# Turns of the logits tile issued ahead of the copies: other turns stand between the turning of a tile and its router product

## The chip, the cores and the metric

The kernel runs on one core of a Trainium2 chip. Its time is the device time of one execution in microseconds (us). The profile is one execution of the same program with the hardware profiler on. The engines are PE (TensorE, matrix products and transposes), DVE (VectorE), ACT (ScalarE), POOL (GpSimd) and SP (SyncE, which here only issues transfers).

## The reference, cut to what matters

The program is one encoder layer on 2048 rows of width 1024, followed by a mixture of experts. The part that the change touches is the *mixing stage*: the outcome of the convolution is normed, the state-space outcome is gated, both are projected and added to the input, and of the new rows the router's logits are computed.

```python
y = layer_norm(y, ln_g, ln_b)                   # convolution branch: norm over 512 channels
y_conv = jax.nn.silu(y)
y = jax.nn.gelu(y).astype(u.dtype)              # state-space branch
y_ssm = y * jax.nn.sigmoid(y @ glu_w + glu_b)
y_cat = jnp.concatenate([rms_norm(y_conv, gb[:CONV_WIDTH]),
                         rms_norm(y_ssm, gb[CONV_WIDTH:])], axis=-1)
x = x + y_cat @ w_out[l]
h = rms_norm(x, g_ffn[l])
g_logits = xf @ w_rg.astype(f32) + b_rg.astype(f32)   # 4 groups; xf is h, flat
e_logits = xf @ w_re.astype(f32) + b_re.astype(f32)   # 32 experts
```

## The kernel before, in words

Three stages come one after the other: projection and tables, convolution with the state-space part, then mixing (`mix`, from L1101), and behind them the experts. The mixing stage works in eight steps n = 0 to 7 of 256 rows each, held as channels by rows, and a ninth turn of the loop, n = 8, that only finishes. Each step ends in two tiles of 128 rows: tile q = 2n is the first and q = 2n + 1 the second one of step n. The loop is shifted: in turn n of the loop the front of step n is computed together with the output of step n - 1, that is, of tiles 2n - 2 and 2n - 1. Every engine runs its own list of instructions, written out by hand in this order, and waits on semaphores by number; no scheduler reorders anything.

What PE does in turn n of the loop (`body`, L1673), in steady state:

- `ln_in(n)` (L1581): 8 turns (transposes of 128x128) of the convolution's outcome `conv_in` into the PSUM banks pa and pb, so that DVE can take mean and variance of each row.
- `sums(n-1)` (L1617): in every second turn the ranks of the chosen experts, then four products with one column each for the branch norms of the step before. They write the bank pd, where the logits also stand, and so wait until DVE has read the last logits (`logit_read`).
- `out_tile` (L1637) of tile 2n - 2: 48 products of 512 columns, the output projection.
- `logit` (L1655) of tile 2n - 3: 8 turns of the normed rows `h` into pc and pa; ACT copies both banks to `hT` in SBUF (L1379, a copy of each bank); then 8 products of 36 columns give the logits in pd.
- `ln_out(n)` (L1591): 8 turns of the rows that ACT normed (`yn`), into pb and pc, from which ACT computes the swish (L1345).
- `glu(n)` (L1601): 48 products of 256 columns for the gate, into pa and pb. They read `yg_hi` (a cast by ACT, L1338) and `yg_lo` (a difference by DVE, L1487).
- `out_tile` of tile 2n - 1, and `logit` of tile 2n - 2.

ACT's list has, around the odd tile: norming (L1333), the two copies of the turned tile, the cast of `yg`, the swish. DVE's list has there: `yg_lo`, four adds of the output tile (L1510, L1513), the norm of tile 2n - 2, the reading of the logits (L1528), in turns 3, 5 and 7 the choice of experts for four tiles (`choose`, L1449), and then the lows of both branches (L1491, L1499), four adds, the reading of the next logits, the norm of the second tile, and at the start of the next turn the statistics with their root (L1463) that ACT's norming waits for.

There are four small banks (pa, pb, pc, pd) and four for the output projection. The waits that guard the banks are `glu_sig` (ACT has read the gate from pa or pb), `yn_done` (ACT has read the turned inputs), `yc_done` (ACT has read the turned normed rows), `h_copied` (ACT has copied a turned half of a tile).

Of the kernel before, what the change touches and what calls it, by code (L numbers as in the profile page):

```python
# [25 lines left out]
T8 = 8  # L26
# [1068 lines left out]
def wait(engine, sem, value):  # L1095

    if not isinstance(value, int) or value > 0:
        engine.wait_ge(sem, value)


def mix(nc, scratch, ident, routing, x, w_out, g_branch, glu_w, columns, g_ffn, w_router, b_router):  # L1101
# [3 lines left out]
    with ExitStack() as ctx:  # L1105
# [42 lines left out]
        pa, pb, pc, pd = ps("pa"), ps("pb"), ps("pc"), ps("pd")  # L1148
# [8 lines left out]
        ln_tr, ln_own, ln_scale, yn_done, ln_back = (sem(n) for n in ("ln_tr", "ln_own", "ln_scale", "yn_done", "ln_back"))  # L1157
# [5 lines left out]
        h_turned, h_copied, logit_done, logit_read = (sem(n) for n in ("h_turned", "h_copied", "logit_done", "logit_read"))  # L1163
# [5 lines left out]
        block = ctx.enter_context(nc.Block())  # L1169
        PARAMS = 3  # L1170

        def over_steps(engine, body):
            for n in range(T8 + 1):
                body(n, n % 2)
# [8 lines left out]
        def first(n):  # L1183
            return isinstance(n, int) and n == 0

        def last_step(n):
            return isinstance(n, int) and n == T8
# [6 lines left out]
        def _(sp):  # L1194
# [40 lines left out]
            def body(n, par):  # L1235
# [5 lines left out]
                if not first(n):  # L1241
                    for t in range(2):
# [4 lines left out]
                        if not last_step(n):  # L1247
                            sp.dma_start(x_sb[:, t], x_rows[n][t]).then_inc(x_ld[t], 16)
            over_steps(sp, body)
            for t in range(2):  # L1250
                sp.wait_ge(x2_st[t], 16 * T8)
# [72 lines left out]
        def _(act):  # L1324
# [48 lines left out]
                nc.scalar.activation(h[:, t], x2[:, t], ACT.Square, accum_out=st[:, 3, 3:4]).then_inc(x2_sq, 1)  # L1373

            def logit(q, t):
                for b, bank in enumerate((pc, pa)):
                    act.wait_ge(h_turned, q * 2 + b + 1)
                    wait(act, logit_done, q)
                    nc.scalar.copy(hT[:, 4 * b:4 * b + 4, :].rearrange("p c k -> p (c k)"), bank[:, :]).then_inc(h_copied, 1)  # L1379
# [9 lines left out]
            def body(n, par):  # L1389
# [8 lines left out]
                if not first(n) and not (isinstance(n, int) and n == 1):  # L1398
                    logit(n * 2 - 3, 1)
# [180 lines left out]
        def _(pe):  # L1580
            def ln_in(n):  # L1581
                pe.wait_ge(conv_ld, 16 * (n + 1))
                wait(pe, glu_sig, n * 2)
                if not (isinstance(n, int) and n < 2):
                    pe.wait_ge(h_copied, n * 4 - 6)
                for t, bank in enumerate((pa, pb)):
                    for c in range(CT):
                        last = nc.tensor.transpose(bank[:, c * P:(c + 1) * P], conv_in[:, c, t * P:(t + 1) * P], ident[:, :])
                    last.then_inc(ln_tr, 1)

            def ln_out(n):  # L1591
                pe.wait_ge(yn_done, n + 1)
                wait(pe, yc_done, n * CT)
                for b, bank in enumerate((pb, pc)):
                    for c in (2 * b, 2 * b + 1):
                        for t in range(2):
                            at = (c % 2) * TN + t * P
                            last = nc.tensor.transpose(bank[:, at:at + P], yn[:, t, c * P:(c + 1) * P], ident[:, :])
                    last.then_inc(ln_back, 1)

            def glu(n):  # L1601
                pe.wait_ge(yg_lo_done, n + 1)
                if first(n):
                    pe.wait_ge(w_lo_done, 2)
                for b, bank in enumerate((pa, pb)):
                    if b == 1:
                        pe.wait_ge(yc_done, n * CT + 2)
                    for m in (2 * b, 2 * b + 1):
                        o = bank[:, (m % 2) * TN:(m % 2 + 1) * TN]
                        for c in range(CT):  # L1610
                            ms = slice(m * P, (m + 1) * P)
                            nc.tensor.matmul(o, glu_hi[:, c, ms], yg_hi[:, c], start=c == 0, stop=False)
                            nc.tensor.matmul(o, glu_hi[:, c, ms], yg_lo[:, c], start=False, stop=False)
                            last = nc.tensor.matmul(o, glu_lo[:, c, ms], yg_hi[:, c], start=False, stop=c == CT - 1)
                    last.then_inc(glu_done, 1)

            def sums(n):  # L1617
                if not first(n):
                    pe.wait_ge(logit_read, n * 2 - 1)
                if ranked_in(n + 1):  # L1620
                    rank_of((n - 3) // 2)
                pe.wait_ge(summed, n * 2 + 2)
                for t in range(2):
                    for branch in range(2):
                        last = nc.tensor.matmul(pd[:, 2 * t + branch:2 * t + branch + 1], sq[:, branch, 0, t * P:(t + 1) * P],
                                                ones[:, :], start=True, stop=True)
                last.then_inc(sums_done, 1)
# [24 lines left out]
                            last = nc.tensor.matmul(o[:, :], cat_hi[:, par, k, ts], wo_lo[:, k, sl], start=False, stop=c == CT - 1)  # L1652
                    last.then_inc(out_done, 1)

            def logit(q, t, sums_n):  # L1655
                pe.wait_ge(h_done, q + 1)
                for b, bank in enumerate((pc, pa)):
                    for c in range(4 * b, 4 * b + 4):
                        last = nc.tensor.transpose(bank[:, (c % 4) * P:(c % 4 + 1) * P], h[:, t, c * P:(c + 1) * P], ident[:, :])
                    last.then_inc(h_turned, 1)  # L1660
                if q == 0:
                    pe.wait_ge(params, 16 * PARAMS)
                pe.wait_ge(h_copied, q * 2 + 2)
                pe.wait_ge(sums_read, sums_n)
                wait(pe, rank_read, (sums_n - 2) // 2)
                wait(pe, logit_read, q)
                for c in range(KD):
                    last = nc.tensor.matmul(pd[:, 64:64 + NL], hT[:, c], wr[:, c], start=c == 0, stop=c == KD - 1)
                last.then_inc(logit_done, 1)
# [1 line left out]
            pe.wait_ge(ones_done, 1)  # L1671

            def body(n, par):  # L1673
                if not last_step(n):
                    ln_in(n)
                if not first(n):
                    sums(n - 1)
                    out_tile(n * 2 - 2, n - 1, 0, 1 - par)
                    if not (isinstance(n, int) and n == 1):
                        if not last_step(n):  # L1680
                            pe.wait_ge(yn_done, n + 1)
                        logit(n * 2 - 3, 1, n)
                if not last_step(n):
                    ln_out(n)
                    glu(n)
                if not first(n):
                    out_tile(n * 2 - 1, n - 1, 1, 1 - par)
                    if not last_step(n):
                        pe.wait_ge(yc_done, n * CT + CT)
                        pe.wait_ge(glu_sig, n * 2 + 1)  # L1690
                    logit(n * 2 - 2, 0, n)
            over_steps(pe, body)
            logit(2 * T8 - 1, 1, T8)


G0, U0, G1, U1, D0, D1 = range(6)
# [686 lines left out]
```

## Time and profile before

| | us |
|---|---|
| median of 3 runs | 1797.01 |
| lowest, highest | 1789.78, 1798.05 |
| the profiled execution | 1796.61 |
| its span in the trace | 1795.1 |
| PE busy of the span | 1613.8 (90%) |
| DVE busy | 1131.2 (63%) |
| ACT busy | 824.6 (46%) |
| POOL busy | 632.0 (35%) |

The span is cut into stages by the lines that run: the mixing stage reaches from about 508 us to 873 us, and its steady turns from 583 us on. A row of a timeline gives the start and the length of one group of equal instructions; matmuls are pipelined, and a group's start is when its first one is issued, so that starts are compared with starts. The granted clock (PEclk) is a share of full speed: 1.00 is 2.4 GHz and 0.50 is 1.2 GHz, and a value between is a stretch that had both.

### The profile page before, as it was taken

How to read it: one execution, taken by the hardware profiler on the slowest of the kernel's cores; microseconds unless marked ns; L12 is line 12 of the kernel's file. 1: busy time of each engine (PE TensorE's matmuls, PEld its weight loads, DVE VectorE, ACT ScalarE, POOL GpSimd, SP SyncE). 2: the span in 40 equal slices, each digit the busy share in tenths (PEclk: the TensorE clock that was granted, in tenths of full speed). 3: DMA queues.
4: the chain of work that ended last, by engine and by line, in shares of the span. 5: the costliest groups of instructions: out<-in, count | busy, mean ns of one | idle time of the engine just before them, and what ended most of it. 6: DMA issues, size and time to landing. Idle time of an engine off the chain costs nothing.

```text
span 1795.1 us, 32279 instructions
## 1 busy us (share of the span) xinstructions
PE 1613.8 (90%) x11107; PEld 1484.5 (83%) x11108; DVE 1131.2 (63%) x1689; ACT 824.6 (46%) x1024; POOL 632.0 (35%) x895
## 2 busy tenths in 40 slices
PE   6999999699947999999379999999999999999990
PEld 6989898588946888887269999999999999999990
DVE  6766654365457676665446747654665888655576
ACT  3412221036354333342325646654665877655563
POOL 0777767343334235554342222222222121222210
PEclk9999999889968999998689999999999999999995
DMA  8723342498563234322469878796887999888888
GB/s 278 229 103 126 118 154 72 144 259 269 171 220 118 94 106 131 95 82 94 165 191 335 291 246 286 265 326 193 276 268 270 374 400 389 289 257 288 291 267 342
DMA packets 125955, 398.20 MB, mean 222 GB/s; under 512 B 33470, under 2 KB 60480, under 8 KB 98880
## 3 DMA queue, kind: packets, MB, share of 16 engines
q1 hardware_dynamic: 101712, 329.97, 50.5%
q0 software_dynamic: 20480, 58.84, 13.3%
q10 hardware_dynamic: 3696, 8.50, 1.2%
q8 instruction: 42, 0.69, 0.2%
q14 instruction: 25, 0.20, 0.0%
HBM read 311.27 MB, written 85.99 MB: 221 GB/s over the span
## 4 chain that ended last, share of the span: by engine, by line
PE 41%; DMA 5%; issue 2%; DVE 1%; ACT 1%; DVEq 1%; POOL 0%; SPq 0%; POOLq 0%; ACTq 0%
PE moe_p_y L2285 4%; PE moe_p_y L2288 4%; PE moe_p_y L2286 4%; PE moe_p_g0u L2272 4%; PE moe_p_g0u L2270 4%; PE moe_p_g0u L2271 4%; PE moe_p_x L2262 2%; PE moe_p_u L2272 2%; PE moe_p_g L2272 2%; PE moe_p_u L2270 2%; PE moe_p_g L2270 2%; PE moe_p_g L2271 2%; PE moe_p_u L2271 2%; DMA residual<-moe_y,moe_ids_s 2%; DMA moe_more<-residual 1%
## 5 line engine op out<-in xcount | busy, mean ns | idle before, releaser
L1724 DVE TENSOR_TENSOR expert_lo<-expert_raw,expert_hi 128x2048 fp32r<-128x2048 f32 x192 | 433.1, 2284 | 59.5 <-ACT expert_hi L1720 40.3
L1720 ACT CAST expert_hi<-expert_raw 128x2048 fp32r<-128x2048 f32 x192 | 362.0, 1912 | 16.4 <-DMA expert_raw<-in_experts 8.7
L706 PE MATMUL proj_p_z<-proj_x_hi,proj_w_hi 128*128 128x256 f32 x768 | 224.3, 292 | 13.9 <-DVE proj_x_lo L554 13.9
L707 PE MATMUL proj_p_z<-proj_x_lo,proj_w_hi 128*128 128x256 f32 x768 | 219.9, 286 | 0.0
L708 PE MATMUL proj_p_z<-proj_x_hi,proj_w_lo 128*128 128x256 f32 x768 | 219.7, 286 | 0.0
L2270 PE MATMUL moe_p_g0u<-expert_hi,moe_xh 128*128 128x256 f32 x736 | 211.0, 287 | 1.5 <-DVE moe_xl L2138 1.5
L2271 PE MATMUL moe_p_g0u<-expert_hi,moe_xl 128*128 128x256 f32 x736 | 207.0, 281 | 0.0
L2272 PE MATMUL moe_p_g0u<-expert_lo,moe_xh 128*128 128x256 f32 x736 | 206.9, 281 | 0.0
L706 PEld LDWEIGHTS proj_p_z<-proj_x_hi,proj_w_hi 128*128 128x128 f32 x768 | 150.0, 195 | 20.5 <-issue 19.4
L2028 POOL DMA_INDIRECT residual<-moe_y,moe_ids_s x45 | 74.4, 1654 | 228.5 <-ACT moe_y L2069 228.5
L2285 PE MATMUL moe_p_y<-expert_hi,moe_hh 128*128 128x512 f32 x368 | 153.4, 417 | 0.0
L707 PEld LDWEIGHTS proj_p_z<-proj_x_lo,proj_w_hi 128*128 128x128 f32 x768 | 150.2, 196 | 0.1
L708 PEld LDWEIGHTS proj_p_z<-proj_x_hi,proj_w_lo 128*128 128x128 f32 x768 | 149.9, 195 | 0.0
L2286 PE MATMUL moe_p_y<-expert_lo,moe_hh 128*128 128x512 f32 x368 | 144.8, 393 | 0.0
L2270 PEld LDWEIGHTS moe_p_g0u<-expert_hi,moe_xh 128*128 128x128 f32 x736 | 139.6, 190 | 4.0 <-issue 1.9
L2271 PEld LDWEIGHTS moe_p_g0u<-expert_hi,moe_xl 128*128 128x128 f32 x736 | 141.0, 192 | 2.0
L2272 PEld LDWEIGHTS moe_p_g0u<-expert_lo,moe_xh 128*128 128x128 f32 x736 | 139.5, 190 | 0.0
L2019 POOL DMA_DIRECT2D moe_ids_s<-slot_table x46 | 25.8, 562 | 275.9 <-DMA residual<-moe_y,moe_ids_s 275.5
L2288 PE MATMUL moe_p_y<-expert_hi,moe_hl 128*128 128x512 f32 x368 | 115.8, 395 | 0.0
L1650 PE MATMUL mix_p_out<-mix_wo_hi,mix_cat_hi 128*128 128x512 f32 x256 | 105.6, 412 | 0.0
L2069 ACT ACTIVATE moe_y<-moe_p_y,moe_ids_s 128x512 f32<-128x512 f32 x90 | 60.3, 688 | 97.7 <-PE moe_p_y L2288 55.8
L2144 DVE TENSOR_TENSOR moe_hid<-moe_p_u,moe_sil 128x256 f32<-128x256 f32 x46 | 19.5, 423 | 135.7 <-PE moe_p_u L2272 126.1
(431 smaller groups left out, 4210.0 us busy)
## 6 DMA issues: line engine op xcount, KB each, us to landing
expert_raw<-in_experts SPq DMA_DIRECT2D x192, 1024.0 KB
ffn_input<-mix_h SPq DMA_DIRECT2D x17, 512.0 KB, 3.9
proj_x_sb<-in_x SPq DMA_DIRECT2D x8, 1024.0 KB, 8.7
turns<-proj_turn POOLq DMA_DIRECT2D x16, 512.0 KB, 4.5
cs_tw<-turns SPq DMA_DIRECT2D x16, 512.0 KB, 8.7
mix_x_sb<-in_x SPq DMA_DIRECT2D x16, 512.0 KB, 5.0
residual<-mix_x SPq DMA_DIRECT2D x16, 512.0 KB, 2.7
proj_x_raw<-in_x_turned SPq DMA_DIRECT2D x7, 1024.0 KB, 6.5
```

What stands on the lines that cost most here:

```text
L706: nc.tensor.matmul(o, whi, x_hi[:, half, c], start=start, stop=False)
L707: nc.tensor.matmul(o, whi, x_lo[:, half, c], start=False, stop=False)
L708: return nc.tensor.matmul(o, wlo, x_hi[:, half, c], start=False, stop=stop)
L1650: nc.tensor.matmul(o[:, :], cat_hi[:, par, k, ts], wo_hi[:, k, sl], start=c == 0, stop=False)
L1720: self.nc.scalar.copy(self.hi[:, u], self.raw[:, u]).then_inc(self.hi_done, 1)
L1724: tensor_tensor(self.lo[:, u], self.raw[:, u], self.hi[:, u].bitcast(FP32), ALU.subtract).then_inc(self.lo_done, 1)
L2270: nc.tensor.matmul(out, xh[:, c], w_hi, start=c == 0, stop=False)
L2271: nc.tensor.matmul(out, xl[:, c], w_hi, start=False, stop=False)
L2272: last_mm = nc.tensor.matmul(out, xh[:, c], w_low, start=False, stop=c == KD - 1)
L2285: nc.tensor.matmul(p_y[i][:, :], hh[:, c], w_hi, start=c == 0, stop=False)
L2286: nc.tensor.matmul(p_y[i][:, :], hh[:, c], w_low, start=False, stop=False)
L2288: last_mm = nc.tensor.matmul(p_y[i][:, :], hl[:, c], weights.outer(hi, D0 + i, c), start=False, stop=c == F // P - 1)
```

## The change

`logit` on PE is split into `turn_tile` (the 8 turns) and `logit` (the wait for both copies and the 8 products). Between them now stand other turns: in turns 2 to 7 of the loop, behind the odd tile 2n - 3, those of `ln_out(n)`; behind the even tile 2n - 2, for n = 1 to 6, those of `ln_in(n+1)`, which so far opened the next turn of the loop. For this to be free of conflicts on the banks, the order of the banks changes: an even tile is turned into pa first and then pc, an odd one as before into pc and then pa (`turned_banks`, on PE and for ACT's copies alike); `ln_in` fills pb first and then pa, and waits before pa for the first copy of the tile; `ln_out` fills pb and then pc, and waits before pc for the first copy. The lists of DVE, POOL and SP are unchanged, and of ACT's only the order of the two banks for even tiles. No instruction is added or removed.

```diff
@@ -1169,6 +1169,10 @@
         block = ctx.enter_context(nc.Block())
         PARAMS = 3
 
+        def turned_banks(q):
+
+            return (pc, pa) if q % 2 else (pa, pc)
+
         def over_steps(engine, body):
             for n in range(T8 + 1):
                 body(n, n % 2)
@@ -1373,7 +1377,7 @@
                 nc.scalar.activation(h[:, t], x2[:, t], ACT.Square, accum_out=st[:, 3, 3:4]).then_inc(x2_sq, 1)
 
             def logit(q, t):
-                for b, bank in enumerate((pc, pa)):
+                for b, bank in enumerate(turned_banks(q)):
                     act.wait_ge(h_turned, q * 2 + b + 1)
                     wait(act, logit_done, q)
                     nc.scalar.copy(hT[:, 4 * b:4 * b + 4, :].rearrange("p c k -> p (c k)"), bank[:, :]).then_inc(h_copied, 1)
@@ -1581,9 +1585,9 @@
             def ln_in(n):
                 pe.wait_ge(conv_ld, 16 * (n + 1))
                 wait(pe, glu_sig, n * 2)
-                if not (isinstance(n, int) and n < 2):
-                    pe.wait_ge(h_copied, n * 4 - 6)
-                for t, bank in enumerate((pa, pb)):
+                for t, bank in ((1, pb), (0, pa)):
+                    if t == 0 and n > 1:
+                        pe.wait_ge(h_copied, n * 4 - 7)
                     for c in range(CT):
                         last = nc.tensor.transpose(bank[:, c * P:(c + 1) * P], conv_in[:, c, t * P:(t + 1) * P], ident[:, :])
                     last.then_inc(ln_tr, 1)
@@ -1592,6 +1596,8 @@
                 pe.wait_ge(yn_done, n + 1)
                 wait(pe, yc_done, n * CT)
                 for b, bank in enumerate((pb, pc)):
+                    if b == 1 and n > 1:
+                        pe.wait_ge(h_copied, n * 4 - 5)
                     for c in (2 * b, 2 * b + 1):
                         for t in range(2):
                             at = (c % 2) * TN + t * P
@@ -1652,12 +1658,14 @@
                             last = nc.tensor.matmul(o[:, :], cat_hi[:, par, k, ts], wo_lo[:, k, sl], start=False, stop=c == CT - 1)
                     last.then_inc(out_done, 1)
 
-            def logit(q, t, sums_n):
+            def turn_tile(q, t):
                 pe.wait_ge(h_done, q + 1)
-                for b, bank in enumerate((pc, pa)):
+                for b, bank in enumerate(turned_banks(q)):
                     for c in range(4 * b, 4 * b + 4):
                         last = nc.tensor.transpose(bank[:, (c % 4) * P:(c % 4 + 1) * P], h[:, t, c * P:(c + 1) * P], ident[:, :])
                     last.then_inc(h_turned, 1)
+
+            def logit(q, sums_n):
                 if q == 0:
                     pe.wait_ge(params, 16 * PARAMS)
                 pe.wait_ge(h_copied, q * 2 + 2)
@@ -1671,26 +1679,33 @@
             pe.wait_ge(ones_done, 1)
 
             def body(n, par):
-                if not last_step(n):
+                if n < 2:
                     ln_in(n)
                 if not first(n):
                     sums(n - 1)
                     out_tile(n * 2 - 2, n - 1, 0, 1 - par)
-                    if not (isinstance(n, int) and n == 1):
-                        if not last_step(n):
-                            pe.wait_ge(yn_done, n + 1)
-                        logit(n * 2 - 3, 1, n)
+                if n > 1:
+                    if not last_step(n):
+                        pe.wait_ge(yn_done, n + 1)
+                    turn_tile(n * 2 - 3, 1)
                 if not last_step(n):
                     ln_out(n)
+                if n > 1:
+                    logit(n * 2 - 3, n)
+                if not last_step(n):
                     glu(n)
                 if not first(n):
                     out_tile(n * 2 - 1, n - 1, 1, 1 - par)
                     if not last_step(n):
                         pe.wait_ge(yc_done, n * CT + CT)
                         pe.wait_ge(glu_sig, n * 2 + 1)
-                    logit(n * 2 - 2, 0, n)
+                    turn_tile(n * 2 - 2, 0)
+                    if n + 1 < T8:
+                        ln_in(n + 1)
+                    logit(n * 2 - 2, n)
             over_steps(pe, body)
-            logit(2 * T8 - 1, 1, T8)
+            turn_tile(2 * T8 - 1, 1)
+            logit(2 * T8 - 1, T8)
 
 
 G0, U0, G1, U1, D0, D1 = range(6)
```

The first place is PE's list around odd tile 1 (turn 2 of the loop), before. `mix_h` are the rows that are turned, `mix_hT` the turned tile in SBUF, `mix_yn` the normed rows; a semaphore's number is shared between stages, and what is printed further down as `s_stored` is `summed` in the code.

```order
L1659 MATMUL mix_pc<-ident,mix_h 128x128 [waits mix_h_done,mix_yn_done]
L1659 MATMUL mix_pc<-ident,mix_h 128x128 x3
L1659 MATMUL mix_pa<-ident,mix_h 128x128 x4
L1668 MATMUL mix_pd<-mix_wr,mix_hT 128x36 [waits mix_logit_read,mix_sums_read,mix_h_copied]
L1668 MATMUL mix_pd<-mix_wr,mix_hT 128x36 x7
L1598 MATMUL mix_pb<-ident,mix_yn 128x128 [waits mix_yc_done,mix_yn_done]
L1598 MATMUL mix_pb<-ident,mix_yn 128x128 x3
L1598 MATMUL mix_pc<-ident,mix_yn 128x128 x4
```

And now:

```order
L1665 MATMUL mix_pc<-ident,mix_h 128x128 [waits mix_h_done,mix_yn_done]
L1665 MATMUL mix_pc<-ident,mix_h 128x128 x3
L1665 MATMUL mix_pa<-ident,mix_h 128x128 x4
L1604 MATMUL mix_pb<-ident,mix_yn 128x128 [waits mix_yc_done,mix_yn_done]
L1604 MATMUL mix_pb<-ident,mix_yn 128x128 x3
L1604 MATMUL mix_pc<-ident,mix_yn 128x128 [waits mix_h_copied]
L1604 MATMUL mix_pc<-ident,mix_yn 128x128 x3
L1676 MATMUL mix_pd<-mix_wr,mix_hT 128x36 [waits mix_logit_read,mix_sums_read,mix_h_copied]
L1676 MATMUL mix_pd<-mix_wr,mix_hT 128x36 x7
```

The eight turns of `mix_yn` have moved ahead of the eight products with `mix_wr`; the one that opens pc waits for a copy.

The second place is PE's list behind even tile 2 (turn 2 of the loop), before.

```order
L1659 MATMUL mix_pc<-ident,mix_h 128x128 [waits mix_h_done,mix_glu_sig,mix_yc_done]
L1659 MATMUL mix_pc<-ident,mix_h 128x128 x3
L1659 MATMUL mix_pa<-ident,mix_h 128x128 x4
L1668 MATMUL mix_pd<-mix_wr,mix_hT 128x36 [waits mix_logit_read,mix_sums_read,mix_h_copied]
L1668 MATMUL mix_pd<-mix_wr,mix_hT 128x36 x7
L1588 MATMUL mix_pa<-ident,mix_conv_in 128x128 [waits mix_h_copied,mix_glu_sig,mix_conv_ld]
L1588 MATMUL mix_pa<-ident,mix_conv_in 128x128 x3
L1588 MATMUL mix_pb<-ident,mix_conv_in 128x128 x4
L1625 MATMUL mix_pd<-mix_ones,mix_sq 128x1 [waits s_stored,mix_logit_read]
L1625 MATMUL mix_pd<-mix_ones,mix_sq 128x1 x3
```

And now:

```order
L1665 MATMUL mix_pa<-ident,mix_h 128x128 [waits mix_h_done,mix_glu_sig,mix_yc_done]
L1665 MATMUL mix_pa<-ident,mix_h 128x128 x3
L1665 MATMUL mix_pc<-ident,mix_h 128x128 x4
L1592 MATMUL mix_pb<-ident,mix_conv_in 128x128 [waits mix_glu_sig,mix_conv_ld]
L1592 MATMUL mix_pb<-ident,mix_conv_in 128x128 x3
L1592 MATMUL mix_pa<-ident,mix_conv_in 128x128 [waits mix_h_copied]
L1592 MATMUL mix_pa<-ident,mix_conv_in 128x128 x3
L1676 MATMUL mix_pd<-mix_wr,mix_hT 128x36 [waits mix_logit_read,mix_sums_read,mix_h_copied]
L1676 MATMUL mix_pd<-mix_wr,mix_hT 128x36 x7
L1631 MATMUL mix_pd<-mix_ones,mix_sq 128x1 [waits s_stored,mix_logit_read]
L1631 MATMUL mix_pd<-mix_ones,mix_sq 128x1 x3
```

The eight turns of `mix_conv_in` have moved ahead of the products, and the products of 36 columns now stand directly before those with one column, which wait for DVE to have read the logits.

## Rows read from the trace of the kernel before

**Rows 1.** Windows, tile's turns to next's: length; each engine's busy us (count); PEclk; DMA.

```profile
599.28:622.22 22.94, 22.21 (x129) 19.73 (x128) 13.49 (x21) 10.56 (x17) 8.43 (x6) 0.93 0.24 80
...
660.16:680.57 20.41, 19.63 (x94) 16.41 (x93) 15.59 (x38) 5.13 (x8) 17.72 (x35) 0.83 0.34 115
...
701.92:721.68 19.76, 19.03 (x90) 16.14 (x88) 11.21 (x34) 4.73 (x7) 16.02 (x19) 0.83 0.42 121
721.68:744.55 22.87, 22.14 (x129) 19.67 (x128) 15.59 (x42) 10.56 (x17) 5.52 (x8) 0.93 0.32 81
744.55:761.58 17.03, 16.30 (x94) 13.72 (x92) 14.65 (x38) 4.73 (x7) 14.98 (x27) 1.00 0.37 124
761.58:782.94 21.36, 20.63 (x130) 18.15 (x130) 13.48 (x22) 10.45 (x17) 8.46 (x12) 1.00 0.31 99
782.94:799.49 16.55, 15.82 (x89) 13.36 (x88) 11.17 (x34) 4.73 (x7) 13.66 (x16) 1.00 0.28 96
```

**Rows 2.** What PE waited for from 582 to 862 us (total, times, longest).

```profile
PE mix_pd L1668 <- ACT mix_hT L1379: 9.4, 13, 0.7
PE mix_pd L1668 <- issue: 1.5, 2, 0.8
PE mix_pd L1634 <- DVE routing_logits L1528: 1.1, 1, 1.1
```

**Rows 3.** PE's timeline at odd tile 9 (start, length, engine, line, what).

```profile
761.58 0.60 PE L1659 MATMUL mix_pc<-ident,mix_h 128*128 128x128 f32 x4
762.02 0.60 PE L1659 MATMUL mix_pa<-ident,mix_h 128*128 128x128 f32 x4
763.34 1.98 PE L1668 MATMUL mix_pd<-mix_wr,mix_hT 128*128 128x36 f32 x16 [0.73 <-ACT mix_hT L1379]
765.15 0.64 PE L1598 MATMUL mix_pb<-ident,mix_yn 128*128 128x128 f32 x4
...
765.98 0.37 PE L1612 MATMUL mix_pa<-mix_yg_hi,mix_glu_hi 128*128 128x256 f32 x1
```

**Rows 4.** ACT's timeline at the same tile.

```profile
760.70 0.77 ACT L1333 ACTIVATE mix_yn<-mix_pb,mix_shift,mix_rs 128x512 f32<-128x512 f32 x1
762.22 0.59 ACT L1379 COPY mix_hT<-mix_pc 128x512 f32<-128x512 f32 x1 [0.75 <-PE mix_pc L1659]
762.70 0.59 ACT L1379 COPY mix_hT<-mix_pa 128x512 f32<-128x512 f32 x1
763.18 1.06 ACT L1338 CAST mix_yg_hi<-mix_yg 128x1024 fp32r<-128x1024 f32 x1
```

**Rows 5.** DVE's timeline at the same tile.

```profile
764.27 1.23 DVE L1487 TENSOR_TENSOR mix_yg_lo<-mix_yg,mix_yg_hi 128x1024 fp32r<-128x1024 f32 x1 [3.14 <-ACT mix_yg_hi L1338]
```

**Rows 6.** PE's timeline at even tile 10.

```profile
784.70 1.98 PE L1668 MATMUL mix_pd<-mix_wr,mix_hT 128*128 128x36 f32 x16 [0.73 <-ACT mix_hT L1379]
786.51 0.64 PE L1588 MATMUL mix_pa<-ident,mix_conv_in 128*128 128x128 f32 x4
...
787.41 0.95 PE L1625 MATMUL mix_pd<-mix_ones,mix_sq 128*128 128x1 f32 x8
788.23 0.47 PE L1650 MATMUL mix_p_out<-mix_wo_hi,mix_cat_hi 128*128 128x512 f32 x1
```

**Rows 7.** DVE's timeline at the same tile.

```profile
786.71 0.20 DVE L1528 TENSOR_TENSOR mix_early_logits<-mix_pd,mix_br 128x36 f32<-128x36 f32 x1 [2.04 <-PE mix_pd L1668]
```

**Rows 8.** PE's timeline at odd tile 3 and at the ranks behind tile 4.

```profile
638.79 0.60 PE L1659 MATMUL mix_pc<-ident,mix_h 128*128 128x128 f32 x4
...
664.90 0.79 PE L1634 MATMUL mix_pd<-mix_both,routing_before 128*128 128x128 f32 x2
```

**Rows 9.** DVE's reading of the logits before the ranks behind tile 4.

```profile
664.66 0.18 DVE L1528 TENSOR_TENSOR mix_early_logits<-mix_pd,mix_br 128x36 f32<-128x36 f32 x1
```

**Rows 10.** ACT's norming (second half) before odd tiles 5 and 11.

```profile
677.77 0.77 ACT L1333 ACTIVATE mix_yn<-mix_pb,mix_shift,mix_rs 128x512 f32<-128x512 f32 x1
...
796.82 0.77 ACT L1333 ACTIVATE mix_yn<-mix_pb,mix_shift,mix_rs 128x512 f32<-128x512 f32 x1
```

## The prediction, made before the changed kernel was run

> **What bounds the kernel now.** I read the page's shares first: PE is busy 90% of the span, so only idle or slow time of PE can be won. Then I cut the mixing stage at the start of each tile's turns [rows 1]: a stretch that begins with an even tile takes 16.55 us (17.03 with ranks in it) where the granted clock was 1.00, one that begins with an odd tile 21.36 us, and PE is busy in all but 0.73 us of each. The list of PE's waits [rows 2] says what that 0.73 us is: 15 times PE waits before the 36-column products until ACT has copied the turned tile (13 put down to ACT, 2 to issue). The one other wait is 1.1 us for DVE. So PE bounds this stage, with one hole per tile. But two groups show how close the others follow. At odd tile 9 ACT's norming ended at 761.47 [rows 4] and PE's turns began at 761.58 [rows 3]. At tile 4 DVE's reading of the logits ended at 664.84 [rows 9] and PE's ranks, which wait for it, began at 664.90 [rows 8]; no hole is shown there, because the modelled end of the turns ahead covers it.
>
> **The hole in issue time.** At tile 9 the turns start at 761.58, four of them take 0.44 us (762.02 less 761.58), and the products start at 763.34 [rows 3]: 1.76 us, of which eight turns are 0.88 and the hole is 0.88. (Ends are modelled, hence 0.73 in the view.) The eight turns that move in take 0.83 us (765.15 to 765.98 at tile 9) or 0.90 us (786.51 to 787.41 at tile 10) [rows 3, 6], so they fill it nearly exactly. There are 12 such places: the odd tiles 1 to 11 with `ln_out`, and the even tiles 0 to 10 with `ln_in`. Tiles 12 to 15 keep their holes.
>
> **Do the moved turns hold up the products?** The added wait, before pc (odd) or pa (even), is for the first copy. At tile 9 that copy ends at 762.81 [rows 4]. The four turns into pb would go from 762.46 to about 762.90, so this wait costs nothing. The second four end at about 763.34, when the second copy (ends 763.29) lets the products go. I price both at 0. If ACT were late, they could cost up to the hole that was there before, 0.88 us, since queued behind the waiting turn are only turns and products that would wait for the second copy anyway. The guards that moved along are long met: `ln_in` now needs all four gate reads, but an output tile of 48 products lies between them and it, and its input is loaded one turn of the loop ahead, an order in SP's list that doesn't change.
>
> **Odd tiles: what is late next.** The next group starts 765.15 - 763.34 = 1.81 us after the products. `glu` could then start at 765.15 rather than 765.98. But it reads `yg_lo`: ACT casts `yg_hi` behind its two copies (763.18 to 764.24) [rows 4], and DVE subtracts from 764.27 to 765.50 [rows 5]. These hang on the start of the turns, and do not move. From a release to the start takes 0.05 to 0.06 us (763.29 to 763.34, 664.84 to 664.90). So `glu` starts at 765.56, and the gain is 765.98 - 765.56 = 0.42 us, not 0.83. ACT's swish can begin right behind the cast, but DVE's chain does not wait for it.
>
> **Even tiles: what is late next.** At tile 10 the products start at 784.70 and their successor at 786.51; then come eight turns, and the sums at 787.41 [rows 6]. Those turns gave DVE time to read the logits (786.71 to 786.91) [rows 7], for which the sums wait since they write the same bank. Now the sums stand directly behind the products: they start at 786.91 + 0.06 = 786.97, and the gain is 0.44 us, not 0.90. DVE's and ACT's next work follows from that reading, which has not moved, and ends with the norming at 797.59 [rows 10]. PE's next turns come at 799.49 - 0.44 = 799.05, still behind it.
>
> **Turns 3, 5 and 7 of the loop: nothing.** Here DVE also chooses experts. From the turns of tile 3 (638.79) its reading of tile 4's logits ends 26.05 us later, and ACT's norming for tile 5 ends at 678.54 [rows 8 to 10], 39.75 us later; for tiles 7 and 9 that is 761.47 - 721.68 = 39.79 us [rows 1, 4]. The chain hangs on the copies and the cast, which stay where they were behind the turns. So the gains of tiles 3 and 4 end at the ranks at 664.90. Those of tiles 7 and 8 end at tile 9: its turns began 39.90 us after tile 7's, and the norming allows 39.85. The wait of 1.1 us before the ranks in turn 8 [rows 2] already shows the same for turn 7, so the gain of tile 11 goes there. Five of the twelve places give 0.
>
> **Sum at the same clock.** Three odd tiles (1, 5, 9) x 0.42 = 1.26 us, and four even ones (0, 2, 6, 10) x 0.44 = 1.76 us: 3.0 us. Its bounds are 12 x 0.88 = 10.6 us, if nothing else were late, and 0, if the copies took the hole's place.
>
> **The clock.** In some stretches the granted clock falls to 0.50 for a while. What that costs is the difference of like stretches [rows 1]: tile 1 has 22.94 against 21.36 (1.6 us), tile 7 has 22.87 (1.5, hidden by the chain above), tile 4 has 20.41 against 17.03 (3.4), tile 6 has 19.76 against 16.55 (3.2). What PE did ahead of all of them is a hole and then the 36-column products, 0.88 + 1.81 = 2.7 us of light work; but the same stood ahead of the stretches at 1.00. After the change the light piece of an odd tile is 1.81 + 0.42 = 2.2 us. That of an even one is 1.81, 0.46 of waiting and 0.82 of sums (787.41 to 788.23) [rows 6] in one piece, 3.1 us, where it was 2.7 and 0.8 with eight turns between. I take one slow stretch fewer at the odd tiles, 1.6 us, and no change at the even ones; the price of both ends is in the rivals.
>
> Forecast: the profiled execution took 1796.6 us, 0.4 below the median of the runs and 1.5 above its span. 1796.6 - 3.0 - 1.6 = **1792.0 us**. Later stages are only shifted.
>
> **The rivals.**
> *Fewer slow stretches.* Filled holes keep the clock up at tiles 1, 4 and 6. That is 1.6 + 3.2 + what the chain of DVE and ACT leaves of tile 4's 3.4 (PE was 680.57 - 678.54 = 2.0 us behind the norming [rows 1, 10]), 6.8 together; with the 3.0, 1786.8 us. For it: half of the hole's place becomes full turns. Against it: the light piece at even tiles grows. The Trainium skill, "TensorE: Matmul & The Clock Gate", section "A second HAM failure mode: psum-queue depth-cycling", says that frequent micro-idles between groups of matmuls make the clock oscillate; by that rule this rival would be the forecast. The trace agrees only in kind: a hole of 0.73 us stands ahead of each slow stretch, and as well ahead of others that kept 1.00.
> *All holes pay.* Neither `yg_lo` nor the reading is next: 1796.6 - 10.6 = 1786.0 us. Against it: the distances of 0.06 us.
> *Slower: more slow stretches at even tiles.* The piece of 3.1 us lets the clock fall at two of the four even tiles that kept it (0, 2, 8, 10), at 3.3 us each, the mean of tiles 4 and 6: 1796.6 - 3.0 + 6.6 = 1800.2 us. It decides from the first one (3.3 against 3.0); all four would give 1806.8.
> *No effect.* The wait for the first copy takes the hole's place, or DVE's chain takes all: 1796.6 us.
>
> **How the numbers follow.** Forecast 0.48 (own range 1789 to 1795), fewer slow stretches 0.16, all holes 0.06, slower 0.18, no effect 0.12. The runs of before spread over 8.3 us (1789.78 to 1798.05), one or two slow stretches either way, so the range for 8 in 10 reaches from the best rival to short of the slower one's middle: 1786 to 1799.5. A measurement of this kernel tells about 0.5%, 9 us, from no change. Faster than 1788.0 takes the first two rivals and little of anything else, less their overlap with the spread: 0.17. Slower than 1806.0 takes all four even tiles: 0.04. Within: 0.79.
>
> **What would show it.** Right: PE's waits for copies fall from 15 to four or so; at odd tiles PE waits a few tenths for `yg_lo`, at even tiles for the reading of the logits; stretches at full clock measure 20.9 and 16.1 us in turns without a choice of experts; from tile 7's turns to tile 9's stays at 39.85 us or more; ranks behind tile 4 still start 26.1 us after tile 3's turns. Wrong: PE waits for the first copy, stretches shorten by 0.88, the turns with a choice shorten as the others do, or the clock column differs at three or more tiles.

## The result, and the profile after

The changed kernel takes 1786.95 us (median of 12 runs, 1780.70 to 1793.77), the kernel before 1796.48 us in the 12 runs beside it (1789.78 to 1802.62). The ratio is 0.994, 95% interval 0.9927 to 0.9954: some 10 us or 0.6% faster, where 5 us were forecast (1792.0) in a range of 1786 to 1799.5. The profiled execution took 1784.26 us, with a span of 1782.8 us.

Of the 12.3 us between the spans of the two traces, 8.4 lie ahead of the mixing stage: its first turns begin at 505.02 us and not at 513.43. In the eleven further traces below, of kernels that all have the same first stages, it begins anywhere from 503.13 to 515.83 us; the kernel of before has 513.43 here and 507.58 in its second trace. So that part is chance of a single execution, and below only the mixing stage is compared.

The changed kernel, cut from one tile's turns to the next, tiles 0, 1, 2, 4, 6, 8, 9 and 12 (length, PE busy and count, granted clock, share of the DMA engines, GB/s); they answer to [rows 1]:

```profile
575.02:591.25 16.23, 15.94 (x89) 1.00 0.41 137
591.25:612.19 20.94, 20.71 (x130) 1.00 0.29 96
612.19:629.98 17.79, 17.50 (x90) 0.90 0.46 148
...
650.91:670.27 19.36, 18.02 (x93) 0.91 0.32 110
...
691.23:707.45 16.22, 15.93 (x89) 1.00 0.45 133
...
728.40:749.05 20.65, 19.31 (x93) 0.83 0.32 109
749.05:769.99 20.94, 20.72 (x129) 1.00 0.29 94
...
807.15:827.69 20.54, 18.38 (x85) 0.83 0.22 78
```

Each stretch of an odd tile now takes 20.93 to 20.96 us, and all six have the full clock; before they took 21.36, and two of six 22.9. An even one takes 16.22 at the full clock (16.55 before), but tiles 2, 4 and 8, and tile 12 behind the places that changed, still have a piece of slow clock. What such a piece is shows in windows cut finer, here tile 1 in the trace of before, PE alone:

```profile
599.28:603.20 3.92, 3.19 (x28) 1.00 0.25 67
603.30:606.50 3.20, 3.20 (x17) 0.50 0.00 0
606.70:622.20 15.50, 15.50 (x86) 1.00 0.29 102
```

The granted clock falls to 0.50 behind the hole and the 36-column products, and comes back while PE works on.

PE's waits in the mixing stage (total, times, longest), which answer to [rows 2]:

```profile
PE mix_pd L1640 <- DVE mix_early_logits L1532: 2.7, 2, 1.3
PE mix_pd L1676 <- ACT mix_hT L1383: 1.6, 2, 0.8
PE mix_pd L1640 <- DVE routing_logits L1532: 1.3, 1, 1.3
PE mix_pd L1631 <- DVE mix_early_logits L1532: 1.2, 4, 0.3
PE mix_pa L1618 <- DVE mix_yg_lo L1491: 0.9, 4, 0.2
```

The 15 waits for copies are down to three, those of tiles 12 to 14 (two in the rows above, and one put down to issue). In their place stand waits for DVE: 0.2 us for `yg_lo` at odd tiles, 0.3 us for the reading of the logits at even ones, and 1.3 us before the ranks in each turn that follows a choice of experts. The ranks behind tile 4 start at 656.09 us, 26.11 after tile 3's turns, as before.

PE at odd tile 9, which answers to [rows 3]:

```profile
749.05 0.60 PE L1665 MATMUL mix_pc<-ident,mix_h 128*128 128x128 f32 x4
...
749.93 0.60 PE L1604 MATMUL mix_pb<-ident,mix_yn 128*128 128x128 f32 x4
750.36 0.62 PE L1604 MATMUL mix_pc<-ident,mix_yn 128*128 128x128 f32 x4
750.82 1.97 PE L1676 MATMUL mix_pd<-mix_wr,mix_hT 128*128 128x36 f32 x16
753.02 0.39 PE L1618 MATMUL mix_pa<-mix_yg_hi,mix_glu_hi 128*128 128x256 f32 x1 [0.22 <-DVE mix_yg_lo L1491]
```

And DVE at the same tile, which answers to [rows 5]:

```profile
751.74 1.23 DVE L1491 TENSOR_TENSOR mix_yg_lo<-mix_yg,mix_yg_hi 128x1024 fp32r<-128x1024 f32 x1 [4.91 <-ACT mix_yg_hi L1342]
```

From the turns to the products are 1.77 us, where it was 1.76: the moved turns fill the hole and hold nothing up. From the turns to `glu` are 753.02 - 749.05 = 3.97 us, 4.40 before, and `yg_lo` ends 0.05 us ahead of it.

PE at even tile 10, which answers to [rows 6]:

```profile
769.99 0.60 PE L1665 MATMUL mix_pa<-ident,mix_h 128*128 128x128 f32 x4
...
771.76 1.97 PE L1676 MATMUL mix_pd<-mix_wr,mix_hT 128*128 128x36 f32 x16
774.02 1.05 PE L1631 MATMUL mix_pd<-mix_ones,mix_sq 128*128 128x1 f32 x8 [0.29 <-DVE mix_early_logits L1532]
774.93 0.48 PE L1656 MATMUL mix_p_out<-mix_wo_hi,mix_cat_hi 128*128 128x512 f32 x1
```

The sums start 4.03 us after the turns (4.47 before), and take 0.91 us, not 0.82, since their own start is no longer hidden: the stretch gains 0.33 us.

### The profile page after: what moved, and what is told of

It is laid out like the page before. It is cut to its first block, busy times and chain, and to the rows that moved or that the text cites. A ratio compares the mean times of both kernels' runs of the same rounds, so it can differ in the third digit from the quotient of the medians.

```text
span 1782.8 us, 32279 instructions
## 1 busy us (share of the span) xinstructions
PE 1605.7 (90%) x11107; PEld 1477.0 (83%) x11108; DVE 1131.0 (63%) x1689; ACT 823.0 (46%) x1024; POOL 634.8 (36%) x895
## 4 chain that ended last, share of the span: by engine, by line
PE 37%; DMA 7%; issue 3%; DVE 2%; DVEq 1%; ACT 1%; POOL 0%; POOLq 0%; SPq 0%; ACTq 0%
PE moe_p_y L2300 4%; PE moe_p_y L2303 4%; PE moe_p_y L2301 4%; PE moe_p_g0u L2285 4%; PE moe_p_g0u L2287 4%; PE moe_p_g0u L2286 4%; DMA residual<-moe_y,moe_ids_s 3%; PE moe_p_x L2277 2%; PE moe_p_g L2287 2%; PE moe_p_u L2287 2%; PE moe_p_g L2286 2%; PE moe_p_u L2286 2%; PE moe_p_g L2285 2%; PE moe_p_u L2285 2%; DMA moe_ids_s<-slot_table 1%
```

## The experiments

**The odd half and the even half alone.** In the first only `ln_out` stands between turns and products; in the second only `ln_in`, with the new order of banks.

```diff
 # odd half: as the changed kernel, but in body()
-                if n < 2:
+                if not last_step(n):
                     ln_in(n)
...
                     turn_tile(n * 2 - 2, 0)
-                    if n + 1 < T8:
-                        ln_in(n + 1)
                     logit(n * 2 - 2, n)
 # (ln_in and the order of the banks as before the change)
 # even half: as the changed kernel, but in body()
                     turn_tile(n * 2 - 3, 1)
+                    logit(n * 2 - 3, n)
                 if not last_step(n):
                     ln_out(n)
-                if n > 1:
-                    logit(n * 2 - 3, n)
-                if not last_step(n):
                     glu(n)
```

> Only the odd tiles (1 to 11) are changed: the turns of ln_out stand between the turns of the tile and its products; the even tiles keep the order of before. Theory of the chain (yg_lo next, 0.42 us at tiles 1, 5 and 9, nothing in the turns with a choice of experts) plus fewer slow clock stretches at odd tiles: stretches of odd tiles at full clock 20.94 us as in the changed kernel, no granted clock under 1.00 in any of them, whole kernel 1.3 + 1.6 to 3.2 = 3 to 4.5 us faster (ratio 0.9975 to 0.9983). Rival, all of the gain of the changed kernel comes from holes that pay in full: 6 x 0.88 = 5.3 us (0.997). Rival, the even tiles make the gain: within 0.1% of before.

> Only the even tiles (0 to 10) are changed: ln_in of the next step stands between the turns and the products of the tile, with the changed order of banks; the odd tiles keep the order of before. Theory of the chain: even stretches at full clock 16.22 us (0.33 less), in turns with a choice of experts nothing, odd stretches stay at 21.36 us or fall into a slow one (22.9) about every third time; whole kernel 1.3 us faster plus what the clock does (0.998 to 1.000). Rival, the clock falls less often at even tiles too: two slow stretches of 3.3 us fewer, 8 us faster (0.9955). Rival, the longer piece of light work makes it fall more: slower, 1.002.

Measured: 0.9972 (0.9944 to 1.0001) and 0.9969 (0.9949 to 0.9990). By these ratios each half is worth about half, but the first interval just reaches no change, and the even half gained more than its forecast. In the trace of the odd half, tiles 1, 6 and 8:

```profile
592.08:613.03 20.95, 20.72 (x130) 1.00 0.26 88
...
690.43:710.12 19.69, 18.96 (x89) 0.83 0.43 122
...
731.08:749.96 18.88, 16.72 (x94) 1.00 0.32 112
```

In that of the even half, tiles 0, 2, 3 and 4:

```profile
575.59:594.96 19.37, 19.08 (x89) 0.82 0.43 135
...
616.32:634.10 17.78, 17.49 (x90) 0.90 0.46 148
634.10:657.01 22.91, 22.18 (x129) 0.93 0.20 69
657.01:676.82 19.81, 19.52 (x94) 0.83 0.41 131
```

Odd tiles keep the full clock in the first (6 of 6) and not in the second (3 of 6), as the theory of light pieces has it. With the even half alone every even tile of the trace has a slow piece, as the slower rival would have it; but three of them (2, 6 and 10) are of 0.90, at 17.78 against 16.22, 1.6 us and not the 3.2 of before. For the ratio this one trace (mixing stage 357.3 us against 353.4 and 360.2 of before) says little: its mean clock was 0.940, and that of the twelve runs of this kernel 0.943.

**Both kernels once more.**

> The kernel of before once more, unchanged, to have a second trace of it and to see what no change measures. Ratio 1.000 within 0.15%. If the 8.4 us by which the changed kernel's mixing stage began earlier in its trace is chance, the start of the mixing stage (first turns of conv_in at 513.4 us in the first trace) will lie elsewhere here, somewhere from 505 to 515. If it belongs to the kernel, it will be at 513 to 514 again. Slow stretches of the mixing stage: five to seven of them, at other tiles than in the first trace, if they are not tied to a tile.

> The changed kernel once more, unchanged, for a second trace. Ratio 0.992 to 0.996. Mixing stage from the first turns of conv_in to the turns of tile 15: 348.4 us in the first trace, 353.4 before; here 346 to 350 if the slow stretches are what varies. Odd tiles at full clock without exception by the theory that the shorter light piece (2.2 us against 2.7) keeps the clock; one or two slow ones among them if it was chance.

Measured: 0.9984 (0.9958 to 1.0009) for the kernel of before against itself, so that a difference of 3 us says little, and 0.9948 (0.9927 to 0.9969) for the changed one. In the second trace of before, tiles 0, 2, 5 and 8:

```profile
577.87:597.60 19.73, 18.96 (x90) 0.83 0.40 133
...
618.97:638.69 19.72, 19.00 (x90) 0.83 0.43 134
...
680.30:703.19 22.89, 22.16 (x129) 0.93 0.26 86
...
741.11:759.63 18.52, 16.72 (x94) 1.00 0.33 114
```

Six slow pieces among tiles 0 to 11 (0, 2, 4, 5, 9, 10); the first trace had four (1, 4, 6, 7), and only tile 4 is in both. Tiles 0 to 11 together take 238.15 and 245.82 us in the two traces of before, 232.13 and 231.68 in those of the changed kernel. The second of the changed kernel has slow pieces at tiles 4 and 10 only.

**Dummies in the hole.** The order of before, where nothing useful moves: the hole is filled with 8 turns, then with 8 products of 36 columns, then with 4.

```diff
-                pe.wait_ge(h_copied, q * 2 + 2)
...
+                if q < 12:
+                    for c in range(8):
+                        nc.tensor.transpose(pd[:, 384:384 + P], ident[:, :], ident[:, :])
+                pe.wait_ge(h_copied, q * 2 + 2)
 # the products, 8 and then 4 of them, in place of the turns:
+                        nc.tensor.matmul(pd[:, 384:384 + NL], ident[:, :], wr[:, c], start=True, stop=True)
```

> The order of before, with 8 turns of the identity into an unused corner of pd in the hole of tiles 0 to 11, issued ahead of the wait for the second copy; nothing useful moves, so the stretches at full clock should stay at 21.36 and 16.56 us (0.88 us of dummies in a hole of 0.88). Theory that the light piece (hole and small products) ahead of glu or the output tile lets the clock fall: it shrinks from 2.7 to 1.8 us, so no odd tile with a clock under 1.00 (4 of 12 in two traces of before) and fewer slow even ones (6 of 12); whole kernel 4 to 6 us faster though it does more work (ratio 0.9967 to 0.998). Rival, the gain of the changed kernel is the time of the holes: 1.000. Rival, dummies get in the way: 1.001 to 1.003.

> As the dummy turns, but the hole is filled with 8 products of 36 columns (identity by the router's weights) in place of 8 turns of 128 columns. PE is never idle in the hole in either. Theory that light products are as bad for the clock as a wait: slow stretches as in before (a third of the odd tiles at 22.9, half of the even ones at 19.7), ratio 1.000. Rival, only idle time of PE between groups lets it fall (micro-idles): full clock at the odd tiles, ratio 0.997 as with the dummy turns.

> The run with 8 dummy products did not match the hole: each product of 36 columns is two instructions in the trace, so that 1.71 us of them stood in a hole of 0.88 us. Here it is 4 products (0.86 us), which fill the hole exactly, as the 8 dummy turns did. Theory that light products let the clock fall like idle time does: as before, odd tiles 22.9 us in about a third, even tiles 19.7 in about half, ratio 1.000. Rival, idle time alone does it: all tiles at full clock, 0.993 as with the dummy turns.

Measured, the 8 turns: 0.9934 (0.9905 to 0.9963), as much as the change and more than was expected. Tiles 0, 1, 4 and 5 of its trace:

```profile
579.31:595.89 16.58, 16.58 (x97) 1.00 0.43 144
595.89:617.26 21.37, 21.37 (x137) 1.00 0.26 86
...
655.19:673.63 18.44, 17.43 (x101) 1.00 0.33 116
673.63:695.04 21.41, 21.41 (x136) 1.00 0.31 99
```

All twelve tiles have the full clock, and ten have the very lengths that before had at it; tiles 4 and 8 take 18.4 and 18.5 us, where DVE's chain holds them (21.37 + 18.44 = 39.81 us from tile 3's turns to tile 5's). PE does 96 turns more and the kernel is 12 us faster, though no stretch at full clock got shorter: what a filled hole gives is to the greater part the clock and not the time of the hole.

The 8 products made it slower, 1.0069 (1.0046 to 1.0091). They did not match the hole: each product of 36 columns is two instructions in the trace, so that they took 1.71 us in a hole of 0.88. Tiles 0, 1 and 5:

```profile
573.34:593.91 20.57, 20.57 (x106) 0.83 0.40 128
593.91:617.68 23.77, 23.77 (x145) 0.93 0.19 67
...
681.46:703.60 22.14, 22.14 (x145) 1.00 0.24 79
```

A stretch at the full clock is 0.8 us longer (22.14 against 21.36), and nine of the twelve have a slow piece: here the clock falls behind 3.5 us of narrow products without a pause. With 4 products (0.90 us, the hole exactly) the ratio was 0.9940 (0.9921 to 0.9958); tiles 1, 5 and 6:

```profile
600.28:621.66 21.38, 21.38 (x138) 1.00 0.27 89
...
678.06:702.66 24.60, 24.60 (x137) 0.86 0.28 87
702.66:719.23 16.57, 16.57 (x98) 1.00 0.48 127
```

One slow piece in twelve. So my expectation, that light products are as bad as a wait, is wrong: at the same length of 2.7 us the wait is worse. Without a wait the clock fell in none of twelve stretches behind 1.8 us of 36-column products (the dummy turns), in one behind 2.7 and in nine behind 3.5.

**The cast ahead of the copies.** In ACT's list, on the changed kernel and on the one before.

```diff
                 elif not last_step(n):
                     front1(n)
                     center(n)
+                    split_gelu(n)
...
                 elif not last_step(n):
-                    split_gelu(n)
                     front2(n, par)
```

> The changed kernel, and in ACT's list the cast of yg (split_gelu) stands ahead of the two copies of the odd tile, not behind them. Theory of the chain: yg_lo is then done before or about at the turns, glu starts right behind the products (odd stretches 20.94 to about 20.5 us) and DVE's adds start with the end of the output tile, some 3 us earlier, so that the turns with a choice of experts are bound by PE as the others: even stretches 4 and 8 from 19.4 to 20.7 us down to 16.7 (17 to 20 where the clock falls), no wait before the ranks. Together 6 x 0.4 + 2 x 2.4 + 1.3 = 8.5 us less than the changed kernel, and up to 6 more by the clock: ratio to before 0.987 to 0.991. Rival, DVE or ACT is late elsewhere and nothing comes of it: 0.9945. Rival, the copies are held up by the cast (1.06 us) and the products wait: 0.995 to 1.000.

> The kernel of before with the same move of the cast in ACT's list and nothing else. glu had 0.42 us to spare, so odd stretches stay at 21.36 us; the wait before the ranks goes (1.1 us at turn 7 of the loop) and stretches 4 and 8 are no longer held by the norming; whole kernel 1 to 4 us faster (0.998 to 0.9995). Rival, the turns with a choice cost more than the traces showed: up to 6 us faster (0.9965). Rival, no change or slower since the copies come behind the cast.

Measured: 0.9887 (0.9860 to 0.9914) on the changed kernel, 0.9953 (0.9932 to 0.9973) on the one before, more than even the rival had there. The trace of the first is of its slowest run (1791.48 us; the six others took 1771.70 to 1776.95), so it has more slow pieces than is usual. Tiles 1, 3 and 4 of the changed kernel with the cast ahead:

```profile
602.15:622.69 20.54, 20.54 (x130) 1.00 0.22 78
...
638.91:659.44 20.53, 20.53 (x129) 1.00 0.30 97
659.44:679.24 19.80, 19.51 (x93) 0.83 0.42 134
```

The odd tiles fall to 20.53 us, as the chain through `yg_lo` demands, and PE is busy all through them; the waits of 1.3 us before the ranks fall to 0.3. At tile 4 PE is now busy for 19.51 of 19.80 us: the chain of DVE no longer holds it, the slow clock does. Of the kernel before with the cast ahead, tiles 8 and 9:

```profile
738.44:756.20 17.76, 16.44 (x94) 1.00 0.35 119
756.20:779.27 23.07, 22.25 (x129) 0.93 0.29 92
```

Tile 8 gains 0.8 us against 18.52, and odd tiles with the hole have slow pieces again (2 of 6). This does not explain 7 us: every hole is still there, and yet the time lost to the clock falls by as much (the table below). Why is open.

**The sums between the halves of the output tile.** With the cast ahead, and on the changed kernel alone. It shortens the light piece behind an even tile to the products, without a dummy.

```diff
                 for half in range(2):
+                    if half == 1:
+                        between()
...
-                    sums(n - 1)
-                    out_tile(n * 2 - 2, n - 1, 0, 1 - par)
+                    out_tile(n * 2 - 2, n - 1, 0, 1 - par, between=lambda: sums(n - 1))
```

> The cast-first kernel, and the sums (and ranks) stand between the halves of the output tile, not ahead of it, so that the light piece behind an even tile is the products alone (1.81 us, was 3.1 with the wait for the reading of the logits and the sums). Theory of light pieces: the even stretches keep the full clock (16.22 less 0.29 of waiting, 15.9 to 16.0 us, 16.4 with ranks; in the cast-first trace they were 17.8 and 19.8), so some 6 x 1.8 + 3 x 3.3 less the trace's share = 12 to 18 us less than the cast-first kernel in a like trace, and a few more in the first turn, where PE waited 10 us for the sums' input: ratio to before 0.979 to 0.984. Rival, the clock at even tiles falls for another reason (ranks, choice, a fixed beat): 0.986 to 0.988. Rival, DVE now waits for the sums: slower than cast-first.

> The changed kernel with only the place of the sums changed in the same way (the cast behind the copies as it was). Theory of light pieces together with DVE's chain: even stretches 0, 2, 6, 10 at 15.9 us and full clock, those with a choice of experts behind them (4, 8) held by the norming at 18.4 to 18.9 us with full clock (19.4 to 20.7 in the two traces): 4 to 9 us less than the changed kernel, ratio to before 0.989 to 0.992. Rival: as the changed kernel, 0.9945.

Measured: 0.9827 (0.9808 to 0.9846) with the cast ahead, 1765.51 us; 0.9923 (0.9903 to 0.9942) without. Tiles 0, 4 and 7 of the first, and ACT's first copy at tile 7:

```profile
572.91:588.68 15.77, 15.77 (x90) 1.00 0.40 135
...
645.48:661.81 16.33, 16.33 (x94) 1.00 0.39 130
...
698.23:720.73 22.50, 20.89 (x130) 1.00 0.58 99
```

```profile
699.88 0.58 ACT L1383 COPY mix_hT<-mix_pc 128x512 f32<-128x512 f32 x1 [1.99 <-PE mix_pa L1667]
```

All twelve have the full clock. At tile 7 the first copy came late, 1.65 us behind the start of the turns where 0.64 is usual. The cast did not hold it, since ACT had been idle for 1.99 us; why it came late is open. Of the second, tiles 0, 4 and 9:

```profile
573.93:589.70 15.77, 15.77 (x89) 1.00 0.39 134
...
647.37:666.29 18.92, 16.45 (x94) 1.00 0.34 112
...
742.93:765.04 22.11, 22.11 (x129) 0.92 0.29 96
```

No even tile has a slow piece (0 of 6, against 5 of 12 in the two traces of the changed kernel), and tile 4 is held by DVE's chain at 18.9 us, with PE idle for 2.5 of them. But this trace is of the fastest of six runs (1771.73 us, median 1781.74), and 0.9923 is a little short of the expected gain. Not all of it lies at the even tiles either: from the first turns of the stage to those of tile 0 the two kernels take 65.5 and 65.4 us, where the changed one takes 70.0. These 4.6 us are about what the second kernel gains on the changed one in the runs. So the traces show that the even tiles keep the clock with the shorter piece, but the times do not show what that is worth. The first of the two is the fastest kernel of the study, 1.7% under the one before.

**The clock of every execution.** A trace is one execution, but the span and the mean granted clock are on record for all of them. Span times (1 - clock) is the time lost to the clock. It counts all stages, and also slow time in which PE had nothing to do, so only its differences are read. Means in us:

| kernel (executions) | lost | kernel of before beside it (executions) |
|---|---|---|
| changed, first and second time (12, 12) | 99.7, 98.7 | 106.3 (35), beside the second |
| before, once more (12) | 104.3 | 106.3 (35) |
| odd half, even half (12, 12) | 100.9, 101.4 | 106.3 (35) |
| dummy turns (7) | 90.8 | 107.1 (24) |
| 8 and 4 dummy products (8, 4) | 112.2, 92.0 | 107.1 (24), 103.5 (11) |
| cast ahead, changed and before (7, 12) | 95.9, 99.7 | 107.1 (24) |
| sums later, with the cast and without (5, 6) | 88.2, 92.6 | 103.5 (11) |

The kernel of before itself reads 103.5 to 107.1 in its four groups, so 3 us here is noise. The changed kernel lost 6.6 and 7.6 us less than the 106.3, the larger part of what it gained. Each half alone lost some 5 us less.

## Why the prediction was right and wrong

- *The moved turns fill the hole and hold nothing up*: right, 1.77 us from turns to products.
- *Odd tiles, `yg_lo` is next, 0.42 us*: right, 20.94 against 21.36, and `glu` 3.97 us after the turns (3.98 forecast). Moving the cast made it 20.53.
- *Even tiles, the reading is next, 0.44 us*: right for the sums' start (4.03 us), but the stretch gains 0.33 (16.22 against 16.55), since the sums take 0.09 us longer.
- *Nothing in the turns with a choice*: right. From tile 7's turns to tile 9's are 20.95 + 20.65 = 41.60 us, in the second trace 20.95 + 18.87 = 39.82, where 39.85 was forecast as the least. With the cast ahead it is 20.54 + 19.79 = 40.33 us, slow piece included.
- *Sum at the same clock, 3.0 us*: right. With all twelve tiles at the full clock the order of before takes 231.50 us (the trace of the dummy turns). The changed one takes 228.39 (its second trace), if its slow pieces are replaced by the like stretch at full clock (for tile 4 that of tile 8, 18.87). The difference is 3.1 us.
- *The clock, 1.6 us*: this is the term that was mis-sized. By the same reckoning slow pieces cost the two traces of before 238.15 - 231.50 = 6.7 and 245.82 - 231.50 = 14.3 us, and the two of the changed kernel 3.7 and 3.3. The mean falls by 7.0 us; with the 3.1 that makes 10.1, and the runs gave 10.8 and 9.3 (0.994 and 0.9948 of 1796.5). That they meet so closely is luck with two traces each, which lie 7.7 us apart for before, but the clock of all executions gives 6.6 to 7.6 us as well. I had the direction at the odd tiles, but took the one trace of before, which was a cheap one, for the typical one, and expected a single slow piece to go.
- *Fewer slow stretches, 1786.8 us, a rival with 0.16*: this is what came, in size (1786.95) and in the two terms (3.0 and 6.8 forecast, 3.1 and 7.0 measured). Its way there is half right: the odd tiles keep the clock, but the even tiles 4 and 6, from which it had most of its 6.8, are not shown to fall less often. The forecast's own sign of being wrong, a clock column that differs at three or more tiles, came true: between the first two traces it differs at tiles 1, 2, 4, 6, 7 and 8.
- *Even tiles unchanged*: wrong in the cost, open in the number. In the four kernels' traces with the hole at even tiles (before twice, the odd half, before with the cast ahead) 10 of 24 even tiles have a slow piece; in the four with `ln_in` in it and the sums directly behind (the changed kernel twice, the even half, cast first) 16 of 24. That there are more, as the slower rival said, is not shown, since two of these last four traces (the even half, cast first) are of executions with a lower clock than is usual for their kernels (0.940, means 0.943 and 0.946). But at tiles 0, 2, 6 and 10 eight of nine cost 1.6 us, and with the hole seven of seven cost 3.2. Among odd tiles it is 9 of 24 with the hole (before twice, the even half, before with the cast) and 1 of 36 with `ln_out` in it.
- *The rule of the Trainium skill* ("TensorE: Matmul & The Clock Gate", "A second HAM failure mode: psum-queue depth-cycling"), that micro-idles between groups make the clock oscillate: I gave the rival that it speaks for 0.16. The dummy turns and the four dummy products agree with it, by 12 and 11 us. It does not cover the eight products, where PE never pauses and the clock falls in nine of twelve stretches, nor the cast ahead on the kernel of before, where the holes stay and 7.4 us less are lost to the clock.
- *All holes pay, 10.6 us*: hits the size and is refuted as a cause, since `yg_lo` and the reading do hold PE at the forecast places, and since dummies in the holes gain as much.

Open is why a slow piece at some even tiles lasts half as long as at others (lost are (1 - 0.90) x 17.78 = 1.8 us and (1 - 0.83) x 19.76 = 3.4), and why the kernel of before loses less to the clock with the cast ahead. That the even half alone is as much faster as the odd half is less odd than its one trace makes it look: its twelve executions lost 4.9 us less than before, those of the odd half 5.4.

## What to carry to other kernels

A short hole in a busy TensorE can cost more than its own length, because the granted clock falls behind it: count the pieces below 1.00 in two or more traces before pricing a hole, and compare the mean clock of all executions; one trace is not the typical case. If filling it with dummies alone makes the kernel faster, the clock is what is being paid for; then order the work so that short waits, narrow products and other light work do not follow one another. And ask of each filled hole what is late next: here the row behind it gave the start of the next work to 0.01 us, and the gain to 0.1.

## What the runs showed of the hardware

After a wait of 0.88 us and 1.81 us of 36-column products the granted clock fell from 1.00 to 0.50 (603.30 to 606.50 us in the trace of before) for a while in 19 of 48 stretches. With 0.88 us of turns, or of further narrow products, in place of the wait, it did so in 0 and 1 of 12; with 1.71 us of narrow products, in 9 of 12. A product of 36 columns in float32 is two instructions of 0.11 us.
